# DVE's sums of weight blocks in both MLP products: one unit in an instruction behind each split, in place of two units at once

## The reference, cut to what matters

```
h2 = rms_norm(x, norm_mlp)            # 512 x 2048
u  = relu(h2 @ w_mlp_up)              # 2048 x 8192
x  = x + (u * u) @ w_mlp_down         # 8192 x 2048
```

## Time and profile before

| | |
|---|---|
| median of 3 runs | 2696.74 us (2694.68 to 2697.59) |
| profiled execution | 2695.96 us, its span 2694.2 us |
| PE busy | 99% of the span |
| weight loads (PEld) busy | 92% |
| DVE busy | 74% |
| ACT busy | 45% |
| granted clock of PE, mean | 0.993 of full speed |
| up product | from about 1357 to 2003 us of the span |
| down product | from about 2009 us to the end |

### The profile page before, as it was taken

One profiled execution on the slowest core, in us unless ns is written; L12 is line 12 of the kernel. 1 busy time (PEld: TensorE's weight loads), 2 busy tenths in 40 slices (PEclk: granted clock), 3 DMA queues, 4 the chain that ended last, 5 costly groups with the idle time before them and its releaser, 6 DMA issues.

```text
span 2694.2 us, 48322 instructions
## 1 busy us (share of the span) xinstructions
PE 2656.4 (99%) x18330; PEld 2478.9 (92%) x18330; DVE 1992.6 (74%) x3081; ACT 1206.2 (45%) x1539; POOL 74.2 (3%) x100
## 2 busy tenths in 40 slices
PE   9999999999999999999999999999999999999997
PEld 8999999788888888888899999999989999999997
DVE  4648887677777754434488888888888888888885
ACT  5534443555555552224444444444454444444443
POOL 0000000000000000000000000000000000000001
PEclk9999999999999999999999999999999999999998
DMA  7444444332232235534334444444465656666664
GB/s 250 121 130 127 128 137 123 97 86 77 75 80 79 78 110 144 151 120 156 125 117 163 142 146 159 142 149 157 142 234 168 190 171 170 183 176 173 190 190 108
DMA packets 366510, 381.43 MB, mean 142 GB/s; under 512 B 18368, under 2 KB 345536, under 8 KB 365888
## 3 DMA queue, kind: packets, MB, share of 16 engines
q1 hardware_dynamic: 336400, 311.73, 38.0%
q10 hardware_dynamic: 21168, 47.19, 4.6%
q0 software_dynamic: 8832, 20.97, 4.0%
HBM read 316.91 MB, written 62.91 MB: 141 GB/s over the span
## 4 chain that ended last, share of the span: by engine, by line
PE 96%; DVE 2%; DMA 1%; ACT 1%; issue 0%; SPq 0%; POOL 0%; ACTq 0%; DVEq 0%
PE job L1788 7%; PE job L1791 7%; PE job L1790 7%; PE job L2105 4%; PE job L2107 4%; PE job L2109 4%; PE scores L2105 4%; PE scores L2109 4%; PE scores L2107 4%; PE stats L2107 2%; PE stats L2109 2%; PE stats L2105 2%; PE turned L2105 2%; PE turned L2109 2%; PE turned L2107 2%; PE heads_out L1888 1%
## 5 line engine op out<-in xcount | busy, mean ns | idle before, releaser
L893 ACT ACTIVATE hi<-pair 128x1792 fp32r<-128x1792 f32 x270 | 459.7, 1703 | 715.7 <-PE heads_out L2109 340.6
L1445 DVE TENSOR_TENSOR lo<-pair,hi 128x1792 fp32r<-128x1792 f32 x270 | 546.7, 2025 | 158.4 <-ACT hi L893 158.4
L728 ACT ACTIVATE w_hi<-raw 128x512 fp32r<-128x512 f32 x268 | 168.8, 631 | 354.2 <-PE job L1791 243.2
L2105 PE MATMUL scores<-h,hi 128*128 128x256 f32 x1024 | 291.9, 285 | 12.7 <-DVE lo L1445 6.6
L1185 DVE TENSOR_TENSOR w_lo<-raw,w_hi 128x512 fp32r<-128x512 f32 x268 | 187.0, 699 | 158.2 <-ACT w_hi L728 157.1
L2105 PE MATMUL job<-h,hi 128*128 128x256 f32 x1024 | 291.2, 284 | 4.5 <-DVE lo L1445 4.5
L2109 PE MATMUL scores<-h,lo 128*128 128x256 f32 x1024 | 291.1, 284 | 0.0
L2107 PE MATMUL scores<-h,hi 128*128 128x256 f32 x1024 | 290.9, 284 | 0.0
L2107 PE MATMUL job<-h,hi 128*128 128x256 f32 x1024 | 290.5, 284 | 0.0
L2109 PE MATMUL job<-h,lo 128*128 128x256 f32 x1024 | 290.4, 284 | 0.0
L1788 PE MATMUL job<-a_hi,w_hi 128*128 128x512 f32 x560 | 229.5, 410 | 0.0
(11 more groups left out here) (458 smaller groups left out, 7024.6 us busy)
## 6 DMA issues: line engine op xcount, KB each, us to landing
pair<-in_w_mlp_up SPq DMA_DIRECT2D x256, 256.0 KB, 2.8
pair<-in_w_mlp_down SPq DMA_DIRECT2D x248, 256.0 KB, 3.3
raw<-in_w_in SPq DMA_DIRECT2D x79, 512.0 KB, 4.1
h<-u_rows SPq DMA_DIRECT2D x39, 896.0 KB, 7.5
u_rows<-u_blocks ACTq DMA_DIRECT2D x32, 896.0 KB, 4.2
pair<-in_w_gate SPq DMA_DIRECT2D x84, 256.0 KB, 2.9
raw<-in_w_out SPq DMA_DIRECT2D x64, 256.0 KB, 3.3
sum_rows<-blocks POOLq DMA_DIRECT2D x24, 512.0 KB, 8.7
```

Source lines behind the costliest of these rows:

```text
L728: nc.scalar.activation(into, raw[:, slot, part:part + KU], ACT.Copy).then_inc(hi_ready, 1)
L893: nc.scalar.activation(pair_hi[j % 2], pairs[j][:, :, 1:8], ACT.Copy).then_inc(pair_hi_ready, 1)
L1445: nc.vector.tensor_tensor(pair_lo[j % 2], pairs[j][:, :, 1:8], pair_hi[j % 2].bitcast(F32), ALU.subtract).then_inc(pair_lo_ready, 1)
L2105: nc.tensor.matmul(into, high, slice_of(s, a, 0), start=first, stop=False, skip_group_check=True)
```

## The change

`sum_pairs` goes and `sum_up_pair` takes its place. It makes the sums of one unit, with patterns half as long, and raises each semaphore by 1 where it was 2. In both products it is called behind every split, for unit n+2, ahead of the combination in the up product and behind it (and behind `total`) in the down product; ahead of the loops two calls stand where one stood. Each call waits for the load of its own unit only.

```diff
-            def sum_pairs(n, j):
-
-                t = pair_sets[j // 2]
-                for i in range(2):
-                    if isinstance(n, int) and n >= UPS:
-                        dve.wait_ge(pair_loaded[j + i], down_loads((n - UPS) // 4, j + i))
-                    else:
-                        dve.wait_ge(pair_loaded[j + i], n * 8 + (32 - 8 * j))
-                nc.vector.tensor_tensor(t[:, :, 4:6], t[:, :, 1:3], t[:, :, 0:1].broadcast_to([P, 4, 2, P]),
-                                        ALU.add).then_inc(sums_first, 2)
-                dve.wait_ge(sums_first, n + 2)
-                nc.vector.tensor_tensor(t[:, :, 6], t[:, :, 4], t[:, :, 2], ALU.add).then_inc(sums_second, 2)
-                dve.wait_ge(sums_second, n + 2)
-                nc.vector.tensor_tensor(t[:, :, 7], t[:, :, 6], t[:, :, 3], ALU.add).then_inc(sums_ready, 2)
+            def sum_up_pair(n, j):
+
+                t = pairs[j]
+                if isinstance(n, int) and n >= UPS:
+                    dve.wait_ge(pair_loaded[j], down_loads((n - UPS) // 4, j))
+                else:
+                    dve.wait_ge(pair_loaded[j], n * 8 + (32 - 8 * j))
+                nc.vector.tensor_tensor(t[:, :, 4:6], t[:, :, 1:3], t[:, :, 0:1].broadcast_to([P, 2, 2, P]),
+                                        ALU.add).then_inc(sums_first, 1)
+                dve.wait_ge(sums_first, n + 1)
+                nc.vector.tensor_tensor(t[:, :, 6], t[:, :, 4], t[:, :, 2], ALU.add).then_inc(sums_second, 1)
+                dve.wait_ge(sums_second, n + 1)
+                nc.vector.tensor_tensor(t[:, :, 7], t[:, :, 6], t[:, :, 3], ALU.add).then_inc(sums_ready, 1)
...
                         if q == 3 and u == first_fill:
-                            sum_pairs(GATE_UNITS, 0)
+                            sum_up_pair(GATE_UNITS, 0)
+                            sum_up_pair(GATE_UNITS + 1, 1)
...
             split_pair(GU + 1, 1)
-            sum_pairs(GU + 2, 2)
+            sum_up_pair(GU + 2, 2)
+            sum_up_pair(GU + 3, 3)
             combine_acts(6)
...
             split_acts(7)
-            sum_pairs(GU + 4, 0)
+            sum_up_pair(GU + 4, 0)
+            sum_up_pair(GU + 5, 1)
...
                     split_pair(n, m % 4)
+                    sum_up_pair(n + 2, (m + 2) % 4)
                     if m == 1:
                         combine_early(i * 2 + (GP - 1), 1, blocks)
                         combine_late(i * 2 + (GP - 1), 1, blocks)
                     if m == 5:
                         combine_early(i * 2 + GP, 0, blocks)
                         combine_late(i * 2 + GP, 0, blocks)
-                    if m % 2 == 0:
-                        sum_pairs(n + 2, (m + 2) % 4)
...
                     if g == 0 and j == 2:
                         split_slice(5)
-                    if j % 2 == 0 and n + 2 < down_unit(GROUPS, 0):
-                        sum_pairs(n + 2, (j + 2) % 4)
+                    if n + 2 < down_unit(GROUPS, 0):
+                        sum_up_pair(n + 2, (j + 2) % 4)
```

## The result

| | before | after |
|---|---|---|
| median | 2695.65 us (8 runs) | 2703.51 us (8 runs) |
| range of the runs | 2694.68 to 2697.59 | 2702.95 to 2704.86 |
| profiled execution, its span | 2695.96, 2694.2 | 2703.43, 2701.7 |
| ratio, 95% interval | | 1.0029, 1.0019 to 1.0040 |

The change costs 7.9 us, 0.29%. The forecast was 8.4 more. The spans differ by 7.5 us, and the trace says where each of them lies.

A forecast was written before the change was run, and what follows sets the result against it. PE, busy 99%, bounds the kernel; DVE matters only when a unit of PE waits. Closing groups 9.7, their old losses -1.6, up start -1.2, down start +1.5, steady 0: +8.4 us on 2696.74, so 2705.1 us, range 2699 to 2713.

The forecast's parts named there:

- Closing groups, +9.7: Down product groups 25 to 31: the j=1 slot grows to 7.22 us, PE loses 1.39 us in each of seven.
- The limit of 0.79 us: In the products, a DVE split may be about 0.8 us late; anything beyond goes to PE in full.
- Steady slots, 0: Steady up and down slots: those with the combination run 0.74 us late against 0.8 allowed, so nothing is lost.
- The rival with 0.1 us in each of 56: Combination slots of both products pass the limit by 0.1 us: 5.6 us more, 2710.7 us; chance 14%.
- No low clock from closing stalls: Closing groups: stalls leave PE's clock up; the rival, a low-clock spell behind each, was +12 us, 2717 us, chance 5%.
- DVE's extra time: Both products: two unit sums take 0.33 us more than a double sum, 42 us over 128 pairs, on DVE.
- Up start, -1.2: Start of the up product: PE's 3.31 us stall shrinks by 1.2; down to -4.0 if the low clock stayed away.
- Down start, +1.5: Start of the down product: sums ahead of splits move the stalls' ends by 1.53 us; bounds 0 and +3.2.
- A wrong limit in the closing groups: Closing splits lose nothing because PE has more reserve than 0.8 us: -1.3, 2695.4 us; chance 8%.
- recovered clocks at the starts: Up and down starts win back 9.2 us of low clock: sum -0.8, 2695.9 us, no change; chance 8%.
- a faster kernel: At both starts all five stalls shrink by 1.2 us and the clock never falls: -7.1, 2689.6 us; chance 5%.
- rivals 4 and 6: Both starts regain 9.2 us of clock: alone, 2695.9 us, 8%; with five stalls shrunk by 1.2 us, 2689.6 us, 5%.

The follow-up runs named there:

- the run with the moved sum: Changed kernel, with the unit's sum of slot j=1 in closing groups 25 to 31 made behind the split of j=0; 2694.93 us, ratio to before 0.9997.
- earlier slices on the kernel before: Kernel before, with loads of down slices 4 and 5 issued ahead of the wait for the first down unit's split; 2692.95 us, ratio 0.9994.
- the up start's edit alone: Kernel before, with only the last double sum ahead of the up loop made as two unit sums; 2693.50 us, ratio 0.9994.
- one memset: Changed kernel, plus a memset of 128 elements behind the combination in 31 up product slots; 2702.94 us, ratio to before 1.0028.

## Why the prediction was right, and where it was off

**Closing groups, +9.7: right.** Seven places, 1.35 us each, 9.4 in all; moving one sum per group takes them away. The duration of a unit's sum, read from the gate product as 1.53 us, is 1.52 in the MLP (1822.19 to 1823.71), so the slot of 7.22 came out at 7.21.

**The limit of 0.79 us: right to 0.1.** Its own rows give 1.76 - 0.95 = 0.81. Measured from both sides, nothing is lost at 0.81 late and 0.15 at 1.04, so it lies between 0.81 and 0.89.

**Steady slots, 0: right within the steady parts.** They stand 0.73 late and lose nothing there. The rival with 0.1 us in each of 56 falls. But the last of them in the up product holds back a load; see the down start below.

**No low clock from closing stalls: right.** The clock behind them is 1.00 (2535 to 2540). The rule of the Trainium skill on idleness and the clock (TensorE: Matmul & The Clock Gate, "What's actually happening") that I weighed against this cost nothing here at idle stretches of 1.13 us; behind the long ones at the starts the clock was lower in some executions.

**DVE's extra time: right.** 40 us against 42. The Trainium skill's advice to keep the count of operations low (VectorE: DVE Perf Modes, "Rules for kernel authors") names a cost that exists: three instructions more cost DVE 0.31 us per pair of units (40 us over 128). But the run with the moved sum has the same count and loses nothing; the rule did not decide.

**Up start, -1.2: the stall is right** (3.31 to 2.12 us), and the profile's gain there was 3.6, because the low clock came in the profiled execution of before and not in that of after. I had this as the lower bound, as something the change could do. The runs don't show that it does: with a stall of 3.33 us the clock from 1375 to 1380 was 1.00 in two kernels (double sums in the up product; earlier slices on the kernel before), and with the stall of 2.12 us it was 1.00 in three (the changed kernel, the up start's edit alone, one memset), and between 0.66 and 0.74 in seven others. So 2.4 of the 3.6 is not shown to come from the change: it was the luck of these two profiles, and may differ from one execution to the next.

**Down start, +1.5: the step that was mis-sized.** It came out at +3.2. "Each end moves by 1.53" held for the sums. What it missed is that the stage had to be reached earlier too. The up product ended 3.6 us earlier than before, but slice 4 was rounded only 1.9 us earlier, after 3.32 us of waiting for its transfer. 3.6 - 1.9 = 1.7, plus 1.5, is 3.2. ACT's rounding of slice 4, before and after:

```profile
2016.22 1.70 ACT L1125 ACTIVATE h<-h 128x1792 fp32r<-128x1792 f32 x1 [1.78 <-DMA h<-u_rows]
...
2014.28 1.70 ACT L1125 ACTIVATE h<-h 128x1792 fp32r<-128x1792 f32 x1 [3.32 <-DMA h<-u_rows]
```

SP's queue says where the 1.7 us went. The loads of slices 0 and 1 and of slices 4 to 7, first before, then after:

```profile
1993.22 0.88 SPq L608 DMA_DIRECT2D h<-u_rows  x2
...
2009.53 2.00 SPq L608 DMA_DIRECT2D h<-u_rows  x4
...
1990.34 0.88 SPq L608 DMA_DIRECT2D h<-u_rows  x2
...
2006.70 2.42 SPq L608 DMA_DIRECT2D h<-u_rows  x4
```

The loads of slices 0 and 1 are issued only 2.88 us earlier, not 3.62. They stand on SP's queue behind a weight load that waits for the split of m=6, the one behind the last combination of the up product, and that split is 0.74 us later against PE. The prediction had put loads issued up to 0.74 us later at nothing; at this place it is a step that failed. It is no accident of one execution: from this issue to the start of PE's first stall of the down start it is 9.5 us in all six profiles with unit sums in the up product and no memset, and 10.2 in all five with double ones.

The lead is still 2.83 us at the load of slice 4, so 0.8 was lost by then, and 0.9 between issue and rounding (7.58 us in place of 6.69). These 0.9 are not shown to come from the change: the time from issue to rounding is 6.9 to 8.1 us in the other profiles with the old order of loads, and 7.5 and 7.7 in the two of them with double sums in the up product. One profile is a rough measure of this stage: from the start of the first stall to the end of the fourth it is 31.85 us before, 35.04 after, 33.53 with unit sums in the up product alone, 34.33 with them in the down product alone, but 32.57 with the up start's edit alone, which changes nothing at this place.

Two errors thus cancel in part, which is luck: -3.6 for -1.2 at the up start, +3.2 for +1.5 here. With the closing groups at 9.4 for 9.7 the profiles differ by 7.4 where the sum was 8.4.

**The rivals.** A wrong limit in the closing groups, recovered clocks at the starts and a faster kernel did not come. The 9.2 us that rivals 4 and 6 put on the clock also count low clock while PE was idle; by the distances of matmul starts in the trace of before the low clock cost about 7.6 us. The down start's clock was 0.59, 0.54 and 0.66 in places; it was not regained.

## What to carry to other kernels

Where an engine behind a saturated one works in slots, add up each slot to the next deadline and compare it with how late its result may be; the average load (75% here) and the number of instructions decided nothing in this kernel. One overfull slot out of four, in seven groups, cost all that this change cost, and moving one sum to the slot ahead took it back. A gain ahead of a stage that waits for transfers is only kept as far as the transfers start earlier with it, and a result that PE gets in time can still come late for a load that is issued behind it.

## What the runs showed of the hardware that was not expected

Whether PE's clock falls behind a stall of 2 to 3.3 us is not settled by the stall's length: behind 3.31 us it was 0.50, behind 3.33 us 1.00, and behind 2.12 us 1.00 in three profiles and 0.66 to 0.74 in seven. And a wait of about 0.15 us for each of 31 units, 4.6 us in all, is not in the list of PE's idle stretches, since a matmul's modelled end (0.28 us where the next starts after 0.12) covers it; it shows in the distance of starts four units apart, in the weight loads' busy time and in the number of matmuls of a stretch.
